# A hybrid decoder layer on one core: four ready-made u tiles for each of seven heads instead of three

## What is computed

```python
q, k, v, cb, cc, cx = jnp.split(_rms(x, g) @ w_in, splits, axis=-1)
a = _diff_attention(rms(q), rms(k), v, lam)            # 8 heads, two softmaxes each
c = _short_conv(cb, cc, cx, conv_w)                    # y = B * causal_conv3(C * xc)
x = x + jnp.concatenate([a, c], axis=-1) @ w_out
x = x + _peer(_rms(x, g2), w_q, subkeys, u, v)         # 8 PEER heads, 128 x 128 keys

# _peer, for each token: 8 heads x 16 experts chosen by product keys
ug, vg = jnp.take(u, eb, axis=0), jnp.take(v, eb, axis=0)
act = gelu(einsum("tkd,td->tk", ug, hb)) * gates
return einsum("tk,tkd->td", act, vg)
```

## Time and profile before

| | us |
|---|---|
| median of 3 runs | 2951.54 (2949.37 to 2952.51) |
| the profiled execution | 2950.59 |
| its span | 2948.8 |

### The profile page before, as it was taken

One profiled execution on the slowest core, in us unless ns is written; L12 is line 12 of the kernel. 1 busy time (PEld: TensorE's weight loads), 2 busy tenths in 40 slices (PEclk: granted clock), 3 DMA queues, 4 the chain that ended last, 5 costly groups with the idle time before them and its releaser, 6 DMA issues.

```text
span 2948.8 us, 40510 instructions
## 1 busy us (share of the span) xinstructions
PE 2881.1 (98%) x14881; PEld 2561.8 (87%) x14881; DVE 2371.8 (80%) x3078; ACT 1054.6 (36%) x1375; POOL 1580.1 (54%) x1022
## 2 busy tenths in 40 slices
PE   8999999999999999999999999999999999999998
PEld 6888778778899999999999999999997788777776
DVE  6455778755579898988889898899677999998898
ACT  4122333341334333434333343344233333333332
POOL 1000454400115765665656566587867878877852
PEclk9999999999999999999999999999999999999999
DMA  8998887779878999999999899999999999999998
GB/s 301 335 351 273 264 277 258 251 281 317 299 237 292 352 341 315 332 326 341 318 323 342 302 337 331 335 339 364 334 361 394 413 416 405 417 418 418 419 416 357
DMA packets 332047, 995.33 MB, mean 338 GB/s; under 512 B 65076, under 2 KB 181824, under 8 KB 250496
## 3 DMA queue, kind: packets, MB, share of 16 engines
q1 hardware_dynamic: 183664, 515.94, 47.2%
q0 software_dynamic: 110656, 447.10, 42.0%
q10 hardware_dynamic: 37584, 30.43, 3.2%
HBM read 873.67 MB, written 119.67 MB: 337 GB/s over the span
## 4 chain that ended last, share of the span: by engine, by line
PE 69%; DVE 13%; DMA 10%; issue 4%; ACT 3%; POOL 1%; ACTq 0%; DVEq 0%; SPq 0%; POOLq 0%
PE ps L1976 21%; PE ps L1978 21%; PE ps L1977 21%; DMA v_two<-in_peer_v 10%; PE ps L2217 3%; DVE x_rows L1826 3%; DVE v_lo L1875 2%; ACT v_hi L1300 2%; DVE u_row L1817 1%; DVE x_one L1924 1%; DVE uT_lo L1785 1%; DVE uT_lo L1790 1%; PE ps L2059 1%; PE ps L2075 1%; DVE dots_at L1880 0%
## 5 line engine op out<-in xcount | busy, mean ns | idle before, releaser
L1976 PE MATMUL ps<-hT_hi,uT_hi 128*128 128x384 f32 x2048 | 698.1, 341 | 7.8 <-DVE uT_lo L1785 4.3
L1978 PE MATMUL ps<-h2T_lo,uT_hi 128*128 128x384 f32 x2048 | 686.1, 335 | 0.0
L1977 PE MATMUL ps<-hT_hi,uT_lo 128*128 128x384 f32 x2048 | 685.0, 334 | 0.0
L935 POOL DMA_INDIRECT gate_grid<-gates,grid_cells x256 | 517.1, 2020 | 105.3 <-issue 78.0
L1976 PE MATMUL ps<-v_hi,a_hi 128*128 128x512 f32 x1024 | 405.6, 396 | 32.3 <-DVE v_lo L1875 31.6
L1978 PE MATMUL ps<-v_lo,a_hi 128*128 128x512 f32 x1024 | 402.4, 393 | 0.0
L1977 PE MATMUL ps<-v_hi,a_lo 128*128 128x512 f32 x1024 | 402.4, 393 | 0.0
L1300 ACT ACTIVATE v_hi<-v_two 128x2048 fp32r<-128x2048 f32 x126 | 241.3, 1919 | 446.8 <-PE ps L1978 322.0
L1976 PEld LDWEIGHTS ps<-hT_hi,uT_hi 128*128 128x128 f32 x2048 | 384.7, 188 | 16.7 <-DVE uT_lo L1785 7.7
L1977 PEld LDWEIGHTS ps<-hT_hi,uT_lo 128*128 128x128 f32 x2048 | 384.9, 188 | 1.9
L1978 PEld LDWEIGHTS ps<-h2T_lo,uT_hi 128*128 128x128 f32 x2048 | 384.3, 188 | 0.0
(11 more groups left out here) (210 smaller groups left out, 4940.7 us busy)
## 6 DMA issues: line engine op xcount, KB each, us to landing
v_two<-in_peer_v SPq DMA_DIRECT2D x63, 2048.0 KB, 11.8
u_tile<-in_peer_u SPq DMA_DIRECT2D x65, 1024.0 KB, 7.5
u_tile<-uT_all SPq DMA_DIRECT2D x63, 1024.0 KB, 6.5
near_rows<-in_peer_u SPq DMA_DIRECT2D x25, 1024.0 KB, 8.6
uT_all<-near_turned SPq DMA_DIRECT2D x100, 256.0 KB, 7.0
w_raw<-in_w_in SPq DMA_DIRECT2D x24, 1024.0 KB, 9.0
wc_raw<-in_w_in SPq DMA_DIRECT2D x48, 512.0 KB, 5.7
half_rows<-in_peer_u SPq DMA_DIRECT2D x44, 512.0 KB, 7.1
```

Of the source, the lines that this page charges most:

```text
L935: pool.indirect_dma_start(out=gate_grid, out_offset=bass.IndirectOffsetOnAxis(ap=grid_cells[:, d, col:col + 1], axis=0), in_=gates[:, 2 + ...
L1976: mm(out, a_hi, b_hi, start=first, stop=False)
L1977: mm(out, a_lo, b_hi, start=False, stop=False)
L1978: return mm(out, a_hi, b_lo, start=False, stop=last)
```

## The change

Four tiles (eight halves) are turned in each of the first seven heads instead of three (six halves): 70 ready-made tiles instead of 63. The seven new ones are the odd tiles 113 to 125, all in the sweep's last PEER head. The order of the three half buffers and the waits for them are rewritten, DVE turns the two further halves behind the third and the fourth of before, and SP and POOL load and store them there. The zero writes are spread anew: four instead of eight in the heads, one just behind them, four at the end of the output projection as before, three right behind the inverse roots of the second norm (`norm(1)`), four later as before. Ahead of the first head DVE makes `norm_qk(0, 0)` first, then turns the two halves, then `norm_qk(0, 1)`, then `split_wc(0, 2)`. `SUMS_CAUGHT_UP` goes from 7 to 12.

```diff
-KEPT_BY_POOL = 1 + 3 * (HEADS - 1)
+KEPT_BY_POOL = 1 + 4 * (HEADS - 1)
+USES_A_HEAD = (3, 2, 3)
+HALF_USES = tuple(n * (HEADS - 1) for n in USES_A_HEAD)
+HALF_PLACES = ((THIRD, 0), (LEFT, 0), (RIGHT, 0), (THIRD, 1), (LEFT, 1), (THIRD, 2), (RIGHT, 1), (LEFT, 2))
+TURNED_SINCE = (2, 1, 2, 2, 2, 1, 3, 2)
-DOTS_CAUGHT_UP, SUMS_CAUGHT_UP = 5, 7
+DOTS_CAUGHT_UP, SUMS_CAUGHT_UP = 5, 12
...
-                sp.wait_ge(seg_ready[NEAR], halves_turned(j, i) - 4)
+                sp.wait_ge(seg_ready[NEAR], halves_turned(j, i) - 2 * TURNED_SINCE[i])
                 load_half(half_of_head(i), tile, half)
...
-                    for i in ((), (0,), (1, 2), (3,), (4,), (5,))[p]:
+                    for i in ((), (0,), (1, 2), (3,), (4, 5), (6, 7))[p]:
                         next_half(j, i)
...
             for j in range(HEADS):
-                zero_cells(j)
+                if j % 2 == 1:
+                    zero_cells(j // 2)
...
-                    for i in range(4):
+                    for i in range(6):
                         keep_half(j, i)
...
-                    for i in range(4, 6):
+                    for i in range(6, HALVES_A_HEAD):
                         keep_half(j, i)
...
             store_o(HEADS - 1)
+            zero_cells(HEADS // 2)
             pool.wait_ge(w_ready, 4 * (QKV_CHUNKS + OUT_CHUNKS))
-            for n in range(HEADS, HEADS + 4):
+            for n in range(5, 9):
                 zero_cells(n)
             norm(1)
+            for n in range(9, 12):
+                zero_cells(n)
...
             keep_qkv(chunks - 1)
-            dve.wait_ge(seg_stored[NEAR], 16 * QUADS * NEAR_HEADS)
-            dve.wait_ge(seg_stored[FAR], 16 * QUADS * FAR_QKV)
-            for x in (LEFT, RIGHT):
-                dve.wait_ge(half_in[x], 16 * HALF_LOADS[x])
-                turn_half(x)
-            split_wc(0, 2)
-            for t in range(TB):
-                dve.wait_ge(proj_kept[t], chunks)
...
+            for t in range(TB):
+                dve.wait_ge(proj_kept[t], chunks)
             norm_qk(0, 0)
+            dve.wait_ge(seg_stored[NEAR], 16 * QUADS * NEAR_HEADS)
+            dve.wait_ge(seg_stored[FAR], 16 * QUADS * FAR_QKV)
+            for x in (LEFT, RIGHT):
+                dve.wait_ge(half_in[x], 16 * HALF_LOADS[x])
+                turn_half(x)
             norm_qk(0, 1)
+            split_wc(0, 2)
...
                 if not last:
                     turn_half_of_head(j, 2)
+                    turn_half_of_head(j, 3)
...
                 if not last:
-                    turn_half_of_head(j, 3)
+                    turn_half_of_head(j, 4)
+                    turn_half_of_head(j, 5)
...
-                    turn_half_of_head(j, 4)
-                    turn_half_of_head(j, 5)
+                    turn_half_of_head(j, 6)
+                    turn_half_of_head(j, 7)
```

More of the change, by code:

```diff
@@ L87 @@
 LEFT, RIGHT, THIRD = 0, 1, 2
-HALF_USES = 2 * (HEADS - 1)
+USES_A_HEAD = (3, 2, 3)
+HALF_USES = tuple(n * (HEADS - 1) for n in USES_A_HEAD)
+HALF_PLACES = ((THIRD, 0), (LEFT, 0), (RIGHT, 0), (THIRD, 1), (LEFT, 1), (THIRD, 2), (RIGHT, 1), (LEFT, 2))
+TURNED_SINCE = (2, 1, 2, 2, 2, 1, 3, 2)
+HALVES_A_HEAD = len(HALF_PLACES)
 HALF_LOADS = (NEAR_QKV + 3, FAR_QKV + 1, 0)
@@ L504, in odd_of_head @@
         def odd_of_head(j, m):
-            k = NEAR_HEADS + 2 * j + m
+            k = NEAR_HEADS + 3 * j + m
             return 2 * k + 1, k
@@ L521, in half_place @@
         def half_place(j, i):
-            place = extra(j) if i >= 4 else odd_of_head(j, 1 + i // 2)
+            place = extra(j) if i >= 6 else odd_of_head(j, 1 + i // 2)
             return place, i % 2
         def half_of_head(i):
-            return (THIRD, LEFT, RIGHT)[i % 3]
+            return HALF_PLACES[i][0]
         def halves_turned(j, i):
-            return 4 * (NEAR_HEADS + 1) + 2 * (6 * j + i)
+            return 4 * (NEAR_HEADS + 1) + 2 * (HALVES_A_HEAD * j + i)
         @nc_block.sync
@@ L687, in _ @@
             sp.wait_ge(conv_stored, 16 * (HEADS - 1))
-            sp.wait_ge(half_kept[THIRD], 16 * QUADS * HALF_USES)
+            sp.wait_ge(half_kept[THIRD], 16 * QUADS * HALF_USES[THIRD])
             load_mix(MIX_ORDER[1])
@@ L765, in _ @@
             for x in range(3):
-                sp.wait_ge(half_kept[x], 16 * QUADS * (HALF_STORES[x] + HALF_USES))
+                sp.wait_ge(half_kept[x], 16 * QUADS * (HALF_STORES[x] + HALF_USES[x]))
             for i in range(PEER_HEADS - 2):
@@ L900, in _ @@
             store_o(HEADS - 1)
+            zero_cells(HEADS // 2)
             pool.wait_ge(w_ready, 4 * (QKV_CHUNKS + OUT_CHUNKS))
-            for n in range(HEADS, HEADS + 4):
+            for n in range(5, 9):
                 zero_cells(n)
             norm(1)
+            for n in range(9, 12):
+                zero_cells(n)
             pool.wait_ge(keys_used, 1)
-            for n in range(HEADS + 4, ZERO_DMAS):
+            for n in range(12, ZERO_DMAS):
                 zero_cells(n)
@@ L1007, in split_weights @@
                     for x in (LEFT, RIGHT):
-                        act.wait_ge(half_kept[x], 16 * QUADS * (HALF_STORES[x] + HALF_USES))
+                        act.wait_ge(half_kept[x], 16 * QUADS * (HALF_STORES[x] + HALF_USES[x]))
                     nc.scalar.activation((wo0_hi if q == 0 else w_hi[1])[:, :, :], wo_raw0, ACT.Copy).then_inc(w_hi_ready, 1)
@@ L1416, in turn_rows @@
                     elif pair == NEAR:
-                        loads, stores = n - NEAR_OUT + HALF_LOADS[LEFT] + HALF_USES, n - KEPT_BY_POOL
+                        loads, stores = n - NEAR_OUT + HALF_LOADS[LEFT] + HALF_USES[LEFT], n - KEPT_BY_POOL
                     else:
-                        loads, stores = n + 1 + HALF_USES, n
+                        loads, stores = n + 1 + HALF_USES[RIGHT], n
                     dve.wait_ge(seg_in[pair], 16 * loads + 16)
@@ L1439, in turn_half_of_head @@
             def turn_half_of_head(j, i):
-                x, use = half_of_head(i), 2 * j + i // 3
+                x, use = HALF_PLACES[i]
+                use = USES_A_HEAD[x] * j + use
                 dve.wait_ge(half_in[x], 16 * (HALF_LOADS[x] + use) + 16)
@@ L1652, in rest_of_chunk @@
                     for x in (LEFT, RIGHT):
-                        dve.wait_ge(half_kept[x], 16 * QUADS * (HALF_STORES[x] + HALF_USES))
+                        dve.wait_ge(half_kept[x], 16 * QUADS * (HALF_STORES[x] + HALF_USES[x]))
                 turn_rows(NEAR, 3 * c + NEAR_OUT, "out")
```

## The result

The changed kernel takes 2965.78 us (median of five executions; 2962.29 to 2972.47) where the kernel before took 2951.54 beside it: 1.005 times as long, interval 1.0039 to 1.0060. That is slower by 14 us, beyond the upper end of the forecast range. The profiled execution took 2969.78 us, its span 2967.6, so its rows show 19 us of loss where the medians have 14.

The account below looks back on a forecast made before the run. PE's work and waits were taken to bound the kernel, with POOL becoming the bound in the last head. -4.0 - 1 + 0.5 + 5 = +0.5 on the profiled 2950.6, 0.9 below the median, gave 2952 us; range 2937 to 2961.

Parts of the forecast that it names:

- Ahead of the first head: Before the first head: PE's idle 2.29 us and 1.7 us of low clock go; -4.0 us, bounds -4 and -2.5.
- The heads: Eight heads: two more halves each, nearly covered, with more DMA traffic; +0.5 us in all, bounds 0 and 1 in each of seven.
- The sweep's start: Sweep's first tiles: adds catching up at tile 12 remove PE's one wait of 1.9 us; -1 us, bounds -2 and +3.
- The zero writes behind the norm: Behind the second norm: three zero writes lie beside DMA traffic that PE doesn't wait for; 0 to +1 us.
- The last head: Sweep's last PEER head: POOL falls behind PE's shorter step, so the sweep's end moves by +5 us; range -10 to +10.
- my walk: Last PEER head: POOL's instructions followed through one tile, with standing behind DVE operations; 11.8 us a tile, not 9.07.
- The dense stage: Stage after the sweep: starts later or sooner by the same amount and passes the shift on.
- (a): Last head: POOL keeps up and the saved transposes come off; -19.5 us, 2932; chance 0.12.
- (b): Last head: POOL falls behind, but at some 10.1 us a tile; last head -10, sum -14.5, 2937; chance 0.15.
- (f): Last head: DMA fills up, cutting its gain to about -5 even if POOL kept up; 2941; chance 0.03.
- (d): Last head: tiles take 12 us or more, the sweep's end moves by +10 or more; 2958 to 2964; chance 0.15.
- (e): Heads: DMA share of 0.94 delays weights for ACT's next copy, over 1 us each; +7, 2958; chance 0.07.

Follow-up runs that it names:

- experiment 7: The changed kernel with the loads of the fifth and sixth half of each head cut from 512 KB to 16 KB; 2959.44 us, ratio 1.0030.
- a_race_won: The changed kernel with four tiny DVE operations on dead data ahead of the sweep's first add, delaying it; 2961.32 us, ratio 1.0035.
- b_sums12: The kernel before with the adds catching up at tile 12 instead of 7, nothing else; 2952.01 us, ratio 0.9999.
- a7_zeros_old: The changed kernel with the adds catching up at tile 7 and the zero writes where they were before; 2955.93 us, ratio 1.0014.
- experiment 8: The changed kernel with adds catching up at tile 7 and the last PEER head's 32 scatters left out; 2947.93 us, ratio 0.9985.
- a_sums7: The changed kernel with the adds catching up at tile 7 again instead of 12, nothing else; 2961.04 us, ratio 1.0031.
- c_even12: The changed kernel, adds at 7, old zero writes, the seven new ready-made tiles at tile 12 of the first seven PEER heads; 2940.57 us, ratio 0.9967.

## Why the prediction was wrong, step by step

**The bound.** That PE's work and PE's waits set the time was right. What I left out: PE's step in the sweep's start rested on where POOL stood against DVE, and I read POOL's rows in the last head only.

**Ahead of the first head**, -4.0: right in kind, -3.5 alone and -2.9 in the changed kernel, within the bounds. My 1.7 us for the clock was a third of the whole 5 us, in which PE worked only 3.64 us; a third of those is 1.2, and 2.29 + 1.2 gives the 3.5. The idle and the low clock are gone; the transposes start at 299.19, 2.17 us sooner than in the earlier trace rows:

```profile
299.19 1.03 PE L2102 MATMUL ps<-ident,qk_n 128*128 128x128 f32 x8
```

**The heads**, +0.5: +3.1, inside the bounds of 0 to 7 and mis-sized. The reading of DVE's gaps was right (experiment 7 gives 0.0 for everything but the two loads). What I got wrong here is "some 3 us later than now" without a price: the DMA share came out at 0.96, a little over my 0.94, one weight piece in each head reaches ACT 0.4 to 1.3 us later than with short loads, and the copy behind it makes PE late, by 0.4 us a head on average.

**The sweep's start**, -1 with -2 to +3: +8.9. This is the step that failed: the only term far outside its bounds, and 9.9 of the 18.4 us by which the profiled execution lies above my sum. It isn't the whole miss: with the race won, a_race_won loses 1.5 us in tiles 0 to 16 and still takes 2961.32 us, just above the range. I priced the constant by PE's one wait of 1.9 us, and the gain at that place came (b_sums12: -2.1 at tile 9), but was given back (+0.3 in all). What was missing is that the order of two starts 0.1 us apart decides POOL's step for the next tiles. The rule that I had read off, an indirect DMA stands behind a DVE operation that began before it, was applied to the last head and not here, where the earlier trace rows already showed POOL working beside the same operations. I named "a gather held up by a later add" and gave it 3 us without walking the queue: it was the first add and not a later one, the gathers of u and a scatter in each tile stand, and at tile 5 DVE's dot waits 3.94 us and PE 2.8.

**The zero writes behind the norm**, 0 to +1: +1.4, a little above its bound, and +1.0 to +2.0 in the four other kernels that have them. I took them to lie beside traffic that PE doesn't wait for; moved away they give this back (a7_zeros_old +0.1).

**The last head**, +5: +4.9 in the changed kernel, +2.1 to +3.6 in five others. Sign and cause were right, and shown: without scatters the head is 10.9 us shorter. The way there was not as I walked it. I had POOL's 4.5 us in hand gone after two to four tiles; in fact eight tiles ran at 9.2 to 10.1 us and won 5.8 us by tile 119, and then eight took 9.6 to 13.5:

```profile
2110.55 3.70 POOL L943 DMA_INDIRECT gate_grid<-gates,grid_cells  x1 [0.30 <-issue]
2114.56 3.34 POOL L943 DMA_INDIRECT gate_grid<-gates,grid_cells  x1 [0.31 <-issue]
2118.20 1.00 POOL L928 DMA_INDIRECT u_row<-in_peer_u,experts  x1 [0.30 <-issue]
...
2123.97 2.29 DVE L1828 CUSTOM_DVE_ANT_0 u_row<-u_row,h_rows 128x2048 f32<-128x2048 f32 x1 [6.08 <-DMA u_row<-in_peer_u,experts]
```

Two scatters in a row stand behind a dot and an add, the gather of u is late, and DVE waits 6.08 us. POOL's tile takes 9.8 to 13.9 us here, as it meets DVE now one way, now another; its mean over seven, 2104.28 to 2187.07 us, is the 11.8 of my walk. That the total hit +5 is partly luck.

**The dense stage** was to pass the shift on. It added 3.7 us in the profiled execution. Other kernels have -2.5 to +4.1 with the same code, so I can't tell this from scatter; what makes it is open.

**The rivals.** (a), (b) and (f) were wrong, the last by experiment 8. (d) asked for 12 us a tile and +10 in the last head; it was 11.8 over seven tiles and +4.9. (e), a late weight piece ahead of ACT's next copy, was the right mechanism at 0.4 us a head instead of over 1. None of them had the sweep's start. Sum of the profiled execution: -2.9 + 3.1 + 0.1 + 1.4 + 8.9 - 0.3 + 4.9 + 3.7 = 18.9 us.

## What to carry to other kernels

Work taken off the bounding engine is worth its time only where the engines that feed it have room: choose the place by their slack (POOL's waits for DVE: 2.7 us a tile over most of the sweep, none but one in the last head), not by where the old scheme happens to end. When an edit shifts one queue, look for the places where two engines start within some tenths of a microsecond on something they share, and price both orders: the expensive one is a term of its own, with its own bound. And a step of "some us later" on a loading queue needs a price, even if nothing on the bounding engine waits for it by name.

## What the runs showed of the hardware

The prediction's reading holds beyond its rows. In the traces of the kernel before, the changed kernel, a_sums7 and c_even12, a gather that starts 0.2 us or more into a DVE operation with two operands from SBUF takes the rest of that operation and some 0.85 us more, a scatter the rest and 1.46 (medians by line 0.84 to 0.87 and 1.44 to 1.48), beside the dot, the add, L1785 and the short products of L1674 and L1737 alike. Inside the low part of a turned tile, which reads one operand from PSUM, they take 0.94 to 1.00 and 1.57 to 1.62 us, as when alone.

An indirect DMA that starts up to 0.08 us behind the start of DVE's add still takes 1.00 us, and the add 2.38 to 2.40 instead of 2.35; one that starts 0.16 us behind it takes 3.06. The border lies between, in all seventeen profiled executions. The order, once lost, stayed until the doubled dots at tile 5.

From the row behind the dot in which DVE reads its sum (at 888.95 in the kernel before) to the start of the gather pass 0.95 us, in which POOL did six memsets (0.6 us) at no cost. In the changed kernel they are 1.04 us. But for the push of fourteen memsets (1.16), all kernels with the zero writes in their old places have 0.94 to 0.96, all with fewer of them in the heads 1.04 to 1.05, whatever else they change; why those 0.09 us are there, no run shows.
